# A hierarchical-MoE encoder block: issuing the token-row gather of pair p+2 ahead of pair p's result store

## What is computed

```python
def _hier_moe(h, w_rg, b_rg, w_re, b_re, w_gate, w_up, w_down):
    ...
    top_v, top_i = lax.top_k(e_sel, TOP_K_INNER)          # 2 experts of the best group
    top_w = jax.nn.softmax(top_v, axis=-1) * g_w
    ...
        act = (jax.nn.silu(hg) * hu * combine[:, gi, :, None].astype(t.dtype)).astype(t.dtype)
        out = out + jnp.einsum('tef,efd->td', act, w_down[gi]).astype(f32)

h1 = _layernorm(DN_ALPHA * h + mix, ln1_w[i], ln1_b[i])
moe = _hier_moe(h1, ...)
ple = jax.nn.sigmoid(h1 @ w_ple_gate[i] + b_ple_gate[i]) * (p[i] @ w_ple[i])
h = _layernorm(DN_ALPHA * h1 + moe + ple, ln2_w[i], ln2_b[i])
```

## Time and profile before

| | |
|---|---|
| Time, median of 3 runs | 841.33 us (839.35 to 846.03) |
| The profiled execution's own time | 837.95 us |
| Its span, first to last instruction | 836.2 us |
| PE busy | 751.3 us, 90% of the span |
| POOL busy | 163.1 us, 20% |
| Mean granted TensorE clock | 0.959 of full |

### The profile page before, as it was taken

The page is one execution under the profiler, slowest core; times in us unless marked ns, Lnnn a source line. Parts: engine busy times, 40 slices in busy tenths (PEclk is TensorE's granted clock), DMA queues, the critical chain, the costliest instruction groups (busy, mean ns, idle before and its releaser), DMA issues.

```text
span 836.2 us, 9526 instructions
## 1 busy us (share of the span) xinstructions
PE 751.3 (90%) x3719; PEld 503.5 (60%) x3719; DVE 406.3 (49%) x740; ACT 189.4 (23%) x335; POOL 163.1 (20%) x121
## 2 busy tenths in 40 slices
PE   5999999999999999999999997999988687979762
PEld 2987789998888788478544883444444343434320
DVE  6698865776788886642165683121111111101227
ACT  4213325553232232400000601211111111101121
POOL 4924670000224220000000023101000000002052
PEclk9999999999999999999999999999998988989885
DMA  9796322111113222442681734799988989899493
GB/s 306 286 375 155 99 75 80 51 52 51 55 49 100 51 51 64 163 150 102 235 318 50 285 118 153 314 392 365 364 339 346 397 316 417 338 368 362 172 182 121
DMA packets 61815, 172.83 MB, mean 207 GB/s; under 512 B 17058, under 2 KB 39788, under 8 KB 47946
## 3 DMA queue, kind: packets, MB, share of 16 engines
q1 hardware_dynamic: 52324, 141.79, 46.2%
q0 software_dynamic: 8752, 28.28, 10.3%
q10 hardware_dynamic: 694, 2.14, 0.6%
HBM read 155.52 MB, written 24.67 MB: 215 GB/s over the span
## 4 chain that ended last, share of the span: by engine, by line
PE 69%; DMA 17%; DVE 6%; issue 4%; POOL 2%; ACT 1%; SPq 0%; POOLq 0%; DVEq 0%
PE psum L873 30%; DMA arena<-h_rows,info 12%; PE psum L1226 7%; PE psum L1101 7%; PE psum L1150 5%; PE psum L1211 4%; PE psum L1082 3%; DMA ring<-in_w_in_dram 3%; PE psum L1169 2%; DMA arena<-y_rows,rowsU 2%; PE psum L1031 2%; PE psum L1051 1%; POOL y_rows L813 1%; PE psum L1153 1%; PE psum L981 1%
## 5 line engine op out<-in xcount | busy, mean ns | idle before, releaser
L873 PE MATMUL psum<-ring_r 128*128 128x512 f32 (+1 forms) x832 | 214.4, 345 | 4.1 <-DVE arena_r L1638 1.7
L873 PEld LDWEIGHTS psum<-ring_r 128*128 128x128 f32 x832 | 145.3, 191 | 25.3 <-issue 3.9
L873 PE MATMUL psum<-arena_r,ring_r 128*128 128x512 f32 (+1 forms) x416 | 141.0, 376 | 0.0
L1326 ACT COPY arena<-psum 128x512 f32<-128x512 f32 (+4 forms) x104 | 57.8, 579 | 290.0 <-PE psum L1108 110.5
L1211 PE MATMUL psum<-ring,arena 128*64 128x512 f32 x512 | 114.4, 599 | 4.2 <-issue 3.0
L738 POOL TENSOR_TENSOR ring_r<-ring,ring_r 128x2048 fp32r<-128x2048 f32 x16 | 73.9, 4622 | 204.3 <-ACT ring_r L1326 204.2
L873 PEld LDWEIGHTS psum<-arena_r,ring_r 128*128 128x128 f32 x416 | 79.2, 190 | 13.7 <-issue 0.5
L1211 PEld LDWEIGHTS psum<-ring,arena 128*64 128x64 f32 x512 | 40.1, 139 | 74.5 <-issue 73.1
L1226 PE MATMUL psum<-ring,arena 128*64 128x512 f32 x256 | 67.2, 672 | 9.3 <-issue 9.3
L1150 PE MATMUL psum<-arena 128*128 128x256 f32 x256 | 63.7, 396 | 1.4 <-DVE arena L1998 1.4
L813 POOL DMA_INDIRECT y_rows<-arena,storeU x15 | 15.1, 1007 | 239.0 <-DVE arena L2116 239.0
(11 more groups left out here) (280 smaller groups left out, 917.4 us busy)
## 6 DMA issues: line engine op xcount, KB each, us to landing
ring<-in_w_exp_down_dram SPq DMA_DIRECT2D x32, 1024.0 KB, 8.4
ring<-in_w_exp_gate_dram SPq DMA_DIRECT2D x32, 1024.0 KB, 8.9
ring<-in_w_exp_up_dram SPq DMA_DIRECT2D x32, 1024.0 KB, 9.4
ring<-in_w_in_dram SPq DMA_DIRECT2D x18, 1024.0 KB, 5.3
y_rows<-arena POOLq DMA_DIRECT2D x12, 1024.0 KB, 16.9
ring<-in_w_out_ssd_dram SPq DMA_DIRECT2D x4, 1024.0 KB, 4.9
ring<-in_w_out_dram SPq DMA_DIRECT2D x4, 1024.0 KB, 5.0
arena<-in_w_ple_gate_dram SPq DMA_DIRECT2D x4, 1024.0 KB, 9.1
```

Source lines behind the costliest of these rows:

```text
L873: t = mm(o, a, b, start=(first and j == 0), stop=(last and j == 2))
L1326: return nc.scalar.copy(dst, src)
```

## The change

In POOL's loop over the pairs, `rows_fetched(p + 2)` stood behind the waits for `down(p)`'s copies and behind the store of pair p. For p = 1 to 13 it now stands ahead of both. For p = 0 it stays behind the store. The wait inside `rows_fetched` is the same.

```diff
             for p in range(LAST):
                 if p == LAST - 1:
                     pool.wait_ge(s_pe_pl, 4 * NT)
                     for dst, name in ((w_ln2, "ln2_w"), (b_ln2, "ln2_b")):
                         pool.dma_start(dst, aps[name].broadcast_to([P, D])).then_inc(s_ln_in, 16)
+                if 0 < p < LAST - 1:
+                    rows_fetched(p + 2)
                 pool.wait_ge(s_y_act, p + 1)
                 pool.wait_ge(s_y_dve, p + 1)
                 g.indirect_dma_start(
                     out=y_dram, out_offset=bass.IndirectOffsetOnAxis(ap=storeU[:, p:p + 1], axis=0), in_=eout[:, p % 2, :],
                     in_offset=None, bounds_check=ROWS - 1, oob_is_err=False).then_inc(y_st[p % 2], 16)
-                if p + 2 <= LAST:
-                    rows_fetched(p + 2)
+                if p == 0:
+                    rows_fetched(2)
```

## The result

| | before | changed |
|---|---|---|
| Time, median | 840.34 us (836.9 to 846.03, 4 runs) | 804.50 us (802.33 to 805.02, 4 runs) |
| Ratio | | 0.9562, 95% interval 0.9505 to 0.9619 |
| The profiled execution's span | 836.2 us | 800.5 us |
| Mean granted TensorE clock | 0.959 | 0.982 |

The kernel became 4.4% faster. The forecast was 814, most likely 806 to 822 and at the outside 804 to 829.

A forecast was written before the change was run, and what follows sets the result against it. Gathers queued late behind the store were taken to bound the kernel, with DMA close behind. `down(14)` at 757 and a tail to 809 cut the 836.2 us span by 27: 841.3 - 27 = 814, range 806 to 822, outside 804 to 829.

The forecast's parts named there:

- The bound and the lead: Gather queued behind the store: issued early, its lead grows from 5.9 to at least 13.6 us, so no wait remains.
- PE's bound: Pairs without waits take 16.3, 14.7 or 15.6 us, so PE could end `down(14)` at 745 instead of 787.9.
- The lower clock: Behind longer gather waits PE runs at 1.2 GHz, not 2.4; pair 10 lost 2.7 us to this.
- The DMA's bound: From 541 to 782 us, 224 us of DMA work all remain, so `down(14)` ends at 751 at the earliest.
- the stream's end: Weight stream ends at 768: 541 plus 224 us of DMA work plus 3 us of idle engines.
- The tail: Behind `down(14)`: store 14, last gathers landed by about 790, then 18.8 us of sums and layer norm, end 809.
- The whole: Whole kernel: a span of 809 instead of 836.2, 27 us less; time 814 against the median of 841.3.
- A: Rival: DMA engines can't exceed 365 GB/s over pairs, weights take the whole wait's place; 832 to 838 us, 12%.
- B: Rival: PE and DMA bounds alternate badly, half of the idle DMA time stays; 15 us gained, 826 us, 18%.
- C: Rival: gather served last behind full weight queue, landing in 18 us, past the 13.6 lead; 853 us, 3%.
- D: Rival: nothing changes because POOL is held by the earlier wait; excluded but for pair 1, 1%.

The follow-up runs named there:

- e1: The changed kernel, but the gather issued behind the waits for `down(p)`'s copies and ahead of the store only: 818.9 us, ratio 0.9729.
- e9: The kernel before, gathers from pair 5 on at their old place but into unread memory, PE not waiting for them: 806.7 us, ratio 0.9608.
- e3: The changed kernel with DVE's row matrix for the last pair made ahead of pair 14's hidden step: 804.5 us, ratio 0.9573.
- e11: The changed kernel with half of each weight slot loaded from pair 3 on and DVE's row matrix made early: 793.2 us, ratio 0.9452.
- e6: The changed kernel with a second gather of the same rows in pairs 5 to 15, into unread memory: 815.9 us, ratio 0.9736.
- e7: The changed kernel with an extra direct load of 0.52 MB in pairs 5 to 15, into unread memory: 817.9 us, ratio 0.9775.

## Why the prediction was right in direction, and which step failed

**The bound and the lead: right.** The gather was late since it stood behind the end of the pair; with a lead of 13.0 us in pair 10 (13.6 had been worked out for pair 7) no gather is waited for. e1 shows the wait shrinking with the lead, e9 that PE's wait, not the gather's place, held the time: with the wait gone and the gather still late, the time is within 2.2 us of the changed kernel's.

**PE's bound: right but for pair 14.** Forecast from `gate_up(3)` to the end of `down(14)`: 745 - 561.9 = 183. Measured 750.0 - 559.5 = 190.5, of which 3.4 are weight waits. Pairs 3 to 5 last 16.1 (16.3 forecast), even pairs 14.5 (14.7), odd ones 15.6 (15.6). Pair 14 was costed at 13 and lasts 17.8: the gather wait of 6.21 us had hidden DVE's row matrix, which was then late next (2.5 us), and `down(14)` behind it runs at the lower clock (5.35 us where 3.65 is usual). The prediction subtracted a wait without asking what else ended during it. e3 and e11 show its worth: nothing beside the weights, 5.9 us without them.

**The lower clock: right.** Pair 10 had lost 2.9 us to it (2.7 forecast), and the other pairs with long waits 1.6 to 2.9; the granted clock of the stretch rose from 0.93 to 0.99.

**The DMA's bound: the step that failed.** "The stretch holds 0.93 x 241 = 224 us of DMA work. None of this work goes away." It took the busy share for work. The stretch before moved 365 GB/s x 241 us = 88.0 MB. The changed kernel moves 412 GB/s at a share of 1.00, and at that rate 88.0 MB take 213.5 us, some 10 less than 224. In the prediction's sum the weights stood at 421 GB/s, so the excess sat in its last term, "the remaining 30.5 us are 13 stores and 13 gathers, 1.2 us each". The same sum over the changed kernel's 205 us (76.66 MB of weights at 421 are 182.1, the layer-norm rows 2.5) leaves 20.4 us for 12 stores and 12 gathers, 0.85 each, and by bytes (e6) it is 0.7. The queue of the weights in the changed kernel, 545 to 750 us, shows the same from the other side:

```profile
q1 hardware_dynamic: 10529, 76.66, 90.3%
```

This is 76.66 MB in 185 busy us, 414 GB/s. Before, 80.50 MB were busy for 84.6% of 241 us, 204 us or 395 GB/s.

With 10 us less in the sum, the DMA bound for the end of `down(14)` is 741 instead of 751 and falls below PE's, and the stream's end comes 10 us ahead of the forecast 768: with the 2.3 us of scatter that is 755 to 756, as seen above. PE first waits for weights ahead of `gate_up(12)`, 0.31 us, where they had been forecast to run out near pair 10. Up to pair 14 this costs 3.4 us, where the forecast allowed 12 (757 - 745). The forecast of 757 for the end of `down(14)` came out at 750.0, 7 us early: 2.3 of this is the scatter ahead of the stage, and 4.7 what the weight waits stayed below their forecast, after pair 14's extra 4.8 is paid. That the two errors, DMA work too dear and pair 14 too cheap, partly cancel is luck.

**The tail: right.** 52 us behind `down(14)` were forecast, 50.5 measured; store 14, landed under load, went from 4.1 us between its issue and the first last-gather to 6.4 (7 forecast). The first last-gather goes out at 758.0, behind the end of the weight stream, so the weights cost these gathers nothing where 1 us was forecast.

**The whole.** A span of 809 was forecast, 800.5 measured: 7.0 us from the end of `down(14)` and 1.5 from the tail. The range reached down to 804 for scatter and overlap, not because the sum itself was doubted.

**The rivals.** A (the stream can't do better than 365 GB/s) fell at once, with 412. B (half of the idle DMA time stays) too, with a share of 1.00. C (served last, a landing past 13.6 us) did not come: no wait names a gather, even in e6 with two of them in each pair, where they land after 10.3 to 11.4 us. D (POOL held by the earlier wait) neither: the gather of pair 11 went out at 663.70, 6 us ahead of the store of pair 9. By HBM Reference in the Trainium skill, Specifications, there were two figures, 358 GB/s per core and about 425 for a core alone; the 412 to 423 measured here agree with the second.

## What to carry to other kernels

A busy share of DMA engines is not an amount of work: price a stream that is to be packed tighter by all its bytes at the rate of a stretch with a full queue (here 88.0 MB at 421 GB/s, 209 us, where 213.5 were measured and 224 forecast), and give the range its lower end from that. When a wait is removed, look for what else ended during it, since that is the next wait; and when a small gain won't show, take the parallel path away too, as e3 and e11 together did. To learn whether a transfer's lateness or its traffic costs the time, keep the traffic and drop the wait.

## What the runs showed of the hardware

With a burst of one gather and one store in each pair beside a weight queue that did not run empty, the stream moved 410 GB/s over 205 us (e9). Behind a stretch in which it had run empty, the engines were 0.99 busy at 344 GB/s for 8 us (before). Extra indirect gathers of 0.29 MB left the rate of a full stream at 419 GB/s, against 420 without them, so they took the time of their bytes; the kernel as a whole paid 1.04 us for each (e6), and 1.22 us for a direct load of 0.52 MB, which is its bytes (e7). Between store 14 and the first gather that waited for it lay 4.1 us with idle DMA engines, and 6.4 beside the end of the weight stream.
